# Last norm of a two-block network: two of eight tiles moved to GpSimd and ScalarE

## The reference, cut to what matters

```python
def rms_norm(x, g):
    xf = x.astype(jnp.float32)
    y = xf * lax.rsqrt(jnp.mean(xf * xf, axis=-1, keepdims=True) + EPS)
    return (y * g).astype(x.dtype)

def second_block(x, ...):
    ...
    for l in range(DEPTH):
        x, xc = hybrid_layer(l, x, xc, ...)
    return rms_norm(x, final_g)
```

## Time and profile before

| | us |
|---|---|
| median of 3 runs | 2971.12 (2971.03 to 2971.16) |
| the profiled execution | 2970.17 |
| its span | 2968.3 |
| TensorE busy | 2898.1 (98%) |
| VectorE busy | 1487.9 (50%) |
| ScalarE busy | 1153.2 (39%) |
| GpSimd busy | 146.0 (5%) |
| granted TensorE clock | 0.998 |

### The profile page before, as it was taken

The page is one execution under the profiler, slowest core; times in us unless marked ns, Lnnn a source line. Parts: engine busy times, 40 slices in busy tenths (PEclk is TensorE's granted clock), DMA queues, the critical chain, the costliest instruction groups (busy, mean ns, idle before and its releaser), DMA issues.

```text
span 2968.3 us, 38325 instructions
## 1 busy us (share of the span) xinstructions
PE 2898.1 (98%) x15438; PEld 2389.9 (81%) x15438; DVE 1487.9 (50%) x2091; ACT 1153.2 (39%) x1816; POOL 146.0 (5%) x199
## 2 busy tenths in 40 slices
PE   9999999999999999999999999999999999999998
PEld 7778888776788887877888788868888788888776
DVE  5655455546464557366252543263455745453454
ACT  5444333526352345146233431173232643341452
POOL 1000000110000000100000300100001000200100
PEclk9999999999999999999999999999999999999999
DMA  5342332331332222210112221311113022321322
GB/s 182 123 158 106 113 128 86 129 131 37 142 111 88 99 92 71 82 54 26 57 46 77 82 68 57 103 63 59 57 64 107 14 82 86 105 87 65 121 75 85
DMA packets 48844, 260.98 MB, mean 88 GB/s; under 512 B 6872, under 2 KB 7904, under 8 KB 24896
## 3 DMA queue, kind: packets, MB, share of 16 engines
q1 hardware_dynamic: 36288, 213.75, 20.7%
q0 software_dynamic: 12416, 45.25, 4.5%
HBM read 250.50 MB, written 4.28 MB: 86 GB/s over the span
## 4 chain that ended last, share of the span: by engine, by line
PE 90%; DVE 5%; ACT 3%; DMA 1%; issue 1%; POOL 0%; SPq 0%; DVEq 0%; ACTq 0%
PE PS L897 15%; PE PS L898 15%; PE PS L899 15%; PE PS L874 7%; PE PS L876 7%; PE PS L875 7%; PE PS L833 3%; PE PS L835 3%; PE PS L834 3%; DVE SMALL L2546 2%; PE PS L1086 1%; PE PS L1197 1%; PE PS L1179 1%; PE PS L1166 1%; PE PS L944 1%
## 5 line engine op out<-in xcount | busy, mean ns | idle before, releaser
L897 PE MATMUL PS<-HHX,WHX 128*128 128x512 f32 (+1 forms) x1440 | 504.1, 350 | 1.0 <-DVE WLX L2396 1.0
L898 PE MATMUL PS<-HL,WHX 128*128 128x512 f32 (+1 forms) x1440 | 502.9, 349 | 0.0
L1680 ACT ACTIVATE WHX<-W 128x2048 fp32r<-128x2048 f32 (+1 forms) x102 | 174.8, 1714 | 562.5 <-DMA W<-in_w 380.9
L899 PE MATMUL PS<-HHX,WLX 128*128 128x512 f32 (+1 forms) x1008 | 349.8, 347 | 0.0
L2396 DVE TENSOR_TENSOR WLX<-W,WHX 128x2048 fp32r<-128x2048 f32 x60 | 137.5, 2292 | 345.4 <-ACT WHX L1680 345.4
L897 PEld LDWEIGHTS PS<-HHX,WHX 128*128 128x128 f32 x1440 | 272.6, 189 | 38.9 <-DVE WLX L2396 2.2
L898 PEld LDWEIGHTS PS<-HL,WHX 128*128 128x128 f32 x1440 | 272.6, 189 | 34.9
L876 PE MATMUL PS<-HH,WL 128*128 128x512 f32 x672 | 261.4, 389 | 0.0
L875 PE MATMUL PS<-HL,WH 128*128 128x512 f32 x672 | 261.4, 389 | 0.0
L874 PE MATMUL PS<-HH,WH 128*128 128x512 f32 x672 | 261.4, 389 | 0.0
L2396 DVE TENSOR_TENSOR WL<-W,WH 128x2048 fp32r<-128x2048 f32 x68 | 155.6, 2289 | 177.7 <-ACT WH L1680 177.7
(11 more groups left out here) (553 smaller groups left out, 5802.9 us busy)
## 6 DMA issues: line engine op xcount, KB each, us to landing
W<-in_w SPq DMA_DIRECT2D x172, 1024.0 KB, 4.8
XC<-in_wm POOLq DMA_DIRECT2D x12, 1024.0 KB, 5.1
H<-in_wm POOLq DMA_DIRECT2D x12, 1024.0 KB, 6.0
W<-in_wb SPq DMA_DIRECT2D x24, 512.0 KB, 3.3
W<-in_w SPq DMA_DIRECT2D x8, 768.0 KB, 4.0
ARENA<-ARENA POOLq DMA_DIRECT2D x32, 128.0 KB, 2.3
ARENA<-mrow SPq DMA_DIRECT2D x12, 256.0 KB, 3.8
PR<-in_nbias POOLq DMA_DIRECT2D x12, 256.0 KB, 3.1
```

What stands on the lines that cost most here:

```text
L897: pe.matmul(dst, wh[:, s, c], hi[:, k, t0:t1], start=k == 0, stop=False)
L898: pe.matmul(dst, wh[:, s, c], lo[:, k, t0:t1], start=False, stop=False)
L899: mm = pe.matmul(dst, wl[:, s, c], hi[:, k, t0:t1], start=False, stop=k == kb - 1)
L1680: act.activation(dst[:, s, 0:n], W[:, s, 0:n], ACT.Copy).then_inc(wh_ready[s], 1)
```

## The change

Of the eight tiles of the last norm VectorE keeps 0, 1, 2, 3, 6 and 7. For tiles 4 and 5 ScalarE multiplies the channel factors into X, right behind the square of each; GpSimd then multiplies by RST and counts `ml_qs`. The third store (tiles 4 and 5) waits for that count, the others for VectorE's.

```diff
@@ plan_stages
-                     **({"xn": 8} if mode in ("X", "both") else {})},
+                     **({"xn": 6 if mode == "X" else 8} if mode in ("X", "both") else {})},
@@ act_norm
             ins.then_inc(sq_ready, 1)
+            if st.mode == "X" and 4 <= m < 6:
+                act.activation(X[:, m, :], X[:, m, :], ACT.Copy, scale=pc(st.g, m))
@@ dve_norm
-        for k in range(KT):
+        for k in (0, 1, 2, 3, 6, 7) if st.mode == "X" else range(KT):
@@ sp_stage
             for k in range(2, KT + 1, 2):
-                sp.wait_ge(x_normed, st["xn"] - KT + k)
+                if k == 6:
+                    sp.wait_ge(sem("ml_qs"), past("ml_qs", 1) + 8 + 2)
+                else:
+                    sp.wait_ge(x_normed, st["xn"] - 6 + min(k, 6))
                 sp.dma_start(out[:, k - 2:k, :], X[:, k - 2:k, :]).then_inc(sem("stored"), 16)
@@ GpSimd
+    def pool_norm(pool, st):
+
+        pool.wait_ge(rstd_ready, st["rs"] + 1)
+        for k in (4, 5):
+            pool.tensor_tensor(X[:, k, :], X[:, k, :], RST[:, 0:T], ALU.mult).then_inc(sem("ml_qs"), 1)
...
             if st.kind == "mlstm":
                 pool_mlstm(pool, st)
+            if st.kind == "norm" and st.mode == "X":
+                pool_norm(pool, st)
```

## The result

| | before | after |
|---|---|---|
| median of 20 runs, us | 2970.72 (2968.99 to 2974.28) | 2974.56 (2973.00 to 2978.34) |
| profiled execution / its span, us | 2970.17 / 2968.3 | 2974.16 / 2972.0 |
| end of the Exp to end of the span ("tail"), us | 8.45 | 11.87 |

The ratio is 1.0013, interval 1.0008 to 1.0019: 2.4 to 5.6 us slower. The forecast was 2973.3, 2.2 us slower, in a range up to 2974.2. The sign was right and the size too small. Everything ahead of the Exp scatters from one execution to the next: in the profiles of this study the Exp ended anywhere from 2958.66 to 2963.79. `early_memset`, `late_wait`, `rstd_psum`, `write_only`, `one_tile` and `drain_early` ran only that once, so nothing is read from their whole times. The tail grew by 3.42 us; the forecast had 2.24.

The account below looks back on a forecast made before the run. TensorE was busy 98%; in the tail VectorE (1.33 us a pair) and store transfers (1.30) coincided as limits. Store 2's data at 2965.71 plus 3.96 plus 0.87 ended the span at 2970.54, +2.2: 2973.3 us, range 2970.8 to 2974.2.

Parts of the forecast that it names:

- ScalarE's two factor multiplications cost 0: Before the Exp: ScalarE's multiplications for tiles 4 and 5 fit idle time; cost 0, without that cover 1.4 us.
- rival 3: On ScalarE: a table load for Copy and another before Ln, 1.28 us more, 2974.6 us; chance 0.02.
- GpSimd's tile costs VectorE 1.16 us, by turns: Last norm: engines take turns reading SBUF; each GpSimd tile costs VectorE 1.16 us, the two add 2.3 us.
- the case in which GpSimd wins the first turn: Variant of the forecast's turns after the Exp: store 1 goes at 2963.55, store 2 still at 2964.9, same end.
- Rival 1: Last norm: VectorE keeps going and GpSimd is served last; +2.4 us, 2973.5 us; chance 0.12.
- rival 2: Last norm: no collision for this kind of operation, so not slower; -0.1 us, 2971.0 us; chance 0.13.
- The stores are the limit from store 2 on; +2.2 us: Final stores: store 2's data start at 2965.71, three stores' worth follow without a gap, ending 2969.67; span +2.2 us.
- Plus 0.87: the span ends at 2970.54: End of program: the span ends 0.87 us after the stores' last data, at 2970.54 for 2968.3.
- VectorE's 1.33 us are hidden by transfers: Tail: six tiles instead of eight save VectorE 1.33 us, but the DMA engines are already full.

Follow-up runs that it names:

- early_memset: Kernel before plus a one-column GpSimd memset released by the Exp that releases VectorE's normalisations; tail 8.99 us.
- late_wait: Kernel before, with GpSimd at its end only waiting for VectorE's last normalisation, no memset; tail 14.48 us.
- rstd_psum: Changed kernel with the Exp made twice, first into PSUM for VectorE, then into RST for GpSimd; tail 12.04 us from the first Exp.
- write_only: Changed kernel with GpSimd's two multiplications replaced by four 128x512 memsets, so GpSimd only writes SBUF; tail 10.85 us.
- one_tile: Changed kernel with only tile 4 on GpSimd and the other seven on VectorE; tail 10.27 us.
- drain_early: Changed kernel with an explicit drain of GpSimd's queue ahead of its last norm work, where it idles; tail 10.57 us.
- both_removed: Changed kernel with VectorE's factor in PSUM and an early explicit GpSimd drain; tail 8.41 us from the first Exp, ratio 1.0001.
- late_memset: Kernel before plus a one-column GpSimd memset released by VectorE's last normalisation; 2976.39 us, ratio 1.0018, tail 14.49 us.

## Why the prediction was wrong, step by step

- *ScalarE's two factor multiplications cost 0.* Right, as far as the traces show. 0.71 us each, all through at 2949.45; VectorE's addition of tile 5 waited 0.44 us and still ended 1.15 us before its next work. No table load between them and the end, so rival 3 is out. From the last addition to the Exp nothing moved (3.98 us in both kernels).
- *GpSimd's tile costs VectorE 1.16 us, by turns.* Right in kind, a little too high: VectorE's run is 6.17 us for 4.07 in `write_only`, so 2.10 for both tiles where the forecast took 2.3. The forecast for the case in which GpSimd wins the first turn had store 1 at 2963.55 and store 2 at 2964.9; they left at 2963.71 and 2965.04, with an Exp 0.28 us later. Rival 1 (VectorE keeps going) and rival 2 (no collision) are out: GpSimd's first took 1.26 us where rival 1 wanted 4 to 5, and VectorE's longest 1853 ns where rival 2 wanted 746.
- *The stores are the limit from store 2 on; +2.2 us.* Right: last data forecast at 2969.67, found at 2969.8, and `drain_early`, in which nothing else is late, has +2.12. As GpSimd won the first turn, store 1 was late already: first data 4.40 us behind the Exp for 2.28 before, and from there 5.3 to 5.4 us of transfer as before. The 2.12 us are the delay of the first byte.
- *"Plus 0.87: the span ends at 2970.54."* This step failed. The 0.87 us from the last data to the end of the span were carried over from a kernel in which SP's wait was the last thing to end. The change puts GpSimd's queue into that competition: 2963.13 + 8.7 + 0.17 = 2972.0. The step has to be a maximum of the engines' ends, and GpSimd's has a term of 8.64 us that the prediction put at nothing. The trace of before had the row for it, 9207 ns long, in the view of the end of the program. I priced GpSimd's work and its collisions and never asked what its queue does after its last operation. Without any collision the span would, by my estimate, still have ended 2.5 + 8.64 + 0.17 = 11.3 us behind the Exp (`rstd_psum`: 12.04, with GpSimd released 0.63 us later). So even without turns rival 2, "not slower", would have failed: a memset of 0.10 us released by the Exp already ends the program later than before (`early_memset`, 8.99 for 8.45). The miss of 1.18 us (3.42 for 2.24) is the 1.30 that `drain_early` takes back, less the 0.12 by which the stores came earlier than forecast.
- *VectorE's 1.33 us are hidden by transfers.* Right, shown by `both_removed`.

What stays open is why the first drain of GpSimd's queue costs 8.64 us and, in the two kernels that have a second, that one about 0.1. In all of these kernels GpSimd issues DMAs ahead of the first drain and none between the two; whether these are the cause was not isolated. Why the forecast of 2.24 for the tail and the measured 3.42 differ is settled; the medians' 3.84 us (2.4 to 5.6) hold the tail's 3.42 and can't be divided finer than that. The forecast started from a median of 3 runs, 2971.12, for 2970.72 over 20; from there its 2.24 us would have given 2973.0, further off still.

## What to carry to other kernels

Before an idle engine gets work near the end of a program, look at what its queue does after its last operation and compare that end with the last store's: here GpSimd's idle time at the end was hiding 8.64 us. If it must work there, try an explicit drain where it idles, and give VectorE's operation at most one SBUF tensor beside it; the two together gave the tail back in `both_removed`, though no time was won. And where stores follow the normalisation at the speed of the transfers, a faster VectorE changed nothing here; an earlier first byte took 0.2 to 0.5 us off the tail.

## What was not expected of the hardware

- A drain of GpSimd's queue took 8639 ns behind a mere wait and 8764 ns with a memset of 0.10 us in it. In `drain_early` and `both_removed` only the first drain was long; the next was over about 0.1 us behind the work.
- The view of waits named TensorE's queue for the idle time before the end (6.2 us in `late_memset`), in a program whose TensorE had been done for 9 us when that wait began. The long row was GpSimd's drain.
- Eight stores of 256 KB kept the DMA engines busy 7 to 8% longer than the four of 512 KB in the kernel before, for the same bytes (5.58 and 5.65 us for 5.22).
